# Moving the act, att, u and squares tiles by 32 and 160 bytes in SBUF, in a two-block transformer kernel

## What is computed

```python
x = first_block(x, ...)
for l in range(2):
    shift1, scale1, gate1, shift2, scale2, gate2 = split(silu(c) @ ada_w[l] + ada_b[l])
    z = (rms_norm(x) * (1 + scale1) + shift1) @ w_in[l]
    mixed = (g_attn * y_attn + g_conv * y_conv) @ w_out[l]
    x = x + (1 + gate1) * mixed
    f_gate, f_up = split((rms_norm(x) * (1 + scale2) + shift2) @ w_ffn_in[l])
    x = x + (1 + gate2) * ((silu(f_gate) * f_up) @ w_ffn_out[l])
```

## Time and profile before

| what | value |
|---|---|
| median of 3 runs | 1083.2 us |
| the three runs | 1083.2, 1084.77, 1076.28 us |
| the profiled execution | 1082.7 us |
| its span, first to last instruction | 1080.7 us |
| mean granted TensorE clock | 0.997 of full speed |

### The profile page before, as it was taken

One profiled execution on the slowest core, in us unless ns is written; L12 is line 12 of the kernel. 1 busy time (PEld: TensorE's weight loads), 2 busy tenths in 40 slices (PEclk: granted clock), 3 DMA queues, 4 the chain that ended last, 5 costly groups with the idle time before them and its releaser, 6 DMA issues.

```text
span 1080.7 us, 19232 instructions
## 1 busy us (share of the span) xinstructions
PE 1058.1 (98%) x8174; PEld 1008.1 (93%) x8174; DVE 833.2 (77%) x1117; ACT 525.7 (49%) x625; POOL 29.8 (3%) x54
## 2 busy tenths in 40 slices
PE   7999999999999999999999999999999999999998
PEld 6778899999998989989999999999898899999998
DVE  6878599988875899877888886879998676554552
ACT  6554665553434435546544343364365464444341
POOL 5000000000000010000000000000000000000000
PEclk9999999999999999999999999999999999999998
DMA  8567249789892554338599998845441556665451
GB/s 288 159 238 243 81 179 338 264 292 317 292 351 78 196 166 156 117 141 303 186 365 314 327 334 282 282 159 198 161 153 43 205 185 197 193 190 185 158 171 39
DMA packets 137473, 230.37 MB, mean 213 GB/s; under 512 B 7107, under 2 KB 60715, under 8 KB 137389
## 3 DMA queue, kind: packets, MB, share of 16 engines
q1 hardware_dynamic: 135060, 227.05, 61.8%
q0 software_dynamic: 1408, 0.79, 0.4%
q10 hardware_dynamic: 921, 1.32, 0.4%
HBM read 227.29 MB, written 1.06 MB: 211 GB/s over the span
## 4 chain that ended last, share of the span: by engine, by line
PE 72%; DVE 18%; ACT 7%; DMA 2%; issue 1%; SPq 0%; ACTq 0%; DVEq 0%
PE mm L437 67%; DVE lo L1298 7%; DVE cacc L1388 5%; ACT hi L842 3%; PE mm L480 1%; ACT pB L921 1%; DMA raw<-in_w_out_dram 1%; DVE sB L1396 1%; DVE qk L1415 1%; DVE hf L1413 1%; DMA swap<-qk 1%; DVE qk L1414 1%; PE pv L578 1%; DMA raw<-in_w_in_dram 1%; PE pa L544 0%
## 5 line engine op out<-in xcount | busy, mean ns | idle before, releaser
L437 PE MATMUL mm<-act_hi,hi 128*128 128x256 f32 x1760 | 489.8, 282 | 5.0 <-ACT act_hi L910 2.3
L437 PE MATMUL mm<-act_hi,lo 128*128 128x256 f32 x1760 | 484.4, 279 | 0.0
L437 PE MATMUL mm<-act_lo,hi 128*128 128x256 f32 x1760 | 467.6, 279 | 0.0
L1298 DVE TENSOR_TENSOR lo<-raw,hi 128x2048 fp32r<-128x2048 f32 (+1 forms) x159 | 359.6, 2265 | 131.6 <-ACT hi L842 128.8
L842 ACT ACTIVATE hi<-raw 128x2048 fp32r<-128x2048 f32 (+1 forms) x159 | 300.2, 1891 | 245.6 <-PE mm L437 205.0
L437 PEld LDWEIGHTS mm<-act_hi,hi 128*128 128x128 f32 x1760 | 330.2, 188 | 10.0 <-issue 6.4
L437 PEld LDWEIGHTS mm<-act_hi,lo 128*128 128x128 f32 x1760 | 329.9, 187 | 0.3
L437 PEld LDWEIGHTS mm<-act_lo,hi 128*128 128x128 f32 x1760 | 320.3, 188 | 0.0
L437 PE MATMUL mm<-u_hi,hi 128*128 128x256 f32 x608 | 170.5, 280 | 0.0
L437 PE MATMUL mm<-u_lo,hi 128*128 128x256 f32 x608 | 169.9, 279 | 0.0
L437 PE MATMUL mm<-u_hi,lo 128*128 128x256 f32 x608 | 169.7, 279 | 0.0
(11 more groups left out here) (280 smaller groups left out, 907.9 us busy)
## 6 DMA issues: line engine op xcount, KB each, us to landing
ada_raw<-in_ada_w_dram SPq DMA_DIRECT2D x128, 384.0 KB, 5.1
raw<-in_w_ffn_in_dram SPq DMA_DIRECT2D x88, 512.0 KB, 5.3
raw<-in_w_in_dram SPq DMA_DIRECT2D x39, 1024.0 KB, 5.1
raw<-in_w_ffn_out_dram SPq DMA_DIRECT2D x20, 1024.0 KB, 6.3
raw<-in_w_up_dram SPq DMA_DIRECT2D x16, 1024.0 KB, 5.8
raw<-in_w_down_dram SPq DMA_DIRECT2D x16, 1024.0 KB, 7.6
raw<-in_w_out_dram SPq DMA_DIRECT2D x12, 1024.0 KB, 6.8
raw<-in_w_in_dram SPq DMA_DIRECT2D x16, 512.0 KB, 6.0
```

The lines of the kernel that those rows point to most:

```text
L437: ins = pe.matmul(o, w[:, kk, fs], a[:, k, :], start=(k == 0 and i == 0 and f % 2 == 0), stop=(ends and i == len(pairs) - 1), skip_group_c ...
L1298: v(dve.tensor_tensor(lo[:, c % RING, 0:nk, :], raw[:, c % RING, 0:nk, :], hi[:, c % RING, 0:nk, :].bitcast(F32), ALU.subtract), "lo_done")
```

## The change

One padding tile grows from 16 to 24 float32 numbers (64 to 96 bytes), and a new one of 28 numbers (112 bytes, which the rounding to 32 bytes makes 128) stands ahead of the region that `qk1`, the `mixA` and `mixB` tiles, `u_hi` and `u_lo` share:

```diff
         x = sb("x", [P, KD, S])
-        sb("act_pad", [P, 16])
+        sb("act_pad", [P, 24])
         act_hi = sb("act_hi", [P, KD, S], F32R)
         act_lo = sb("act_lo", [P, KD, S], F32R)
...
         tabs = sb("tabs", [P, 2, 2 * S])
 
 
+        sb("mix_pad", [P, 28])
         mixA = ExitStack()
         qk1 = sb("qk1", [P, KD, S], on=mixA)
```

## The result

| what | before | after |
|---|---|---|
| median | 1080.85 us (4 runs, 1076.28 to 1084.77) | 1094.76 us (4 runs, 1094.3 to 1096.2) |
| profiled execution, its span | 1082.7, 1080.7 us | 1094.55, 1092.4 us |

The ratio after to before is 1.0132, with a 95% interval of 1.0086 to 1.0179: the changed kernel is slower, by 1.3%. It lies inside the stated range, but not where the forecast was, which was no change. One more thing stands in the table: the kernel before scatters over 8.5 us, the changed one over 1.9 us.

The account below looks back on a forecast made before the run. The prediction took TensorE's issue pace at L437 to bound the kernel. Every moved tile was costed at 0, so 1082.7 + 0 = 1082.7 us for the profiled execution; it named 1082, range 1050 to 1104.

Parts of the forecast that it names:

- What bounds the kernel: TensorE's issue pace at line L437, about 117.8 ns between starts, 67% of the chain, 724 us; other engines' traffic changes nothing.
- I take 0 ns per matmul for all of them: Matmuls on the moved act, u and att tiles: the new starts add 0 ns each, bounded by 10 less or 7 more.
- The row of `on` at 544: Float32 product at L437, tile at 544 mod 1024: 216 ns beside 215.6 for constants, taken as sign that such starts cost nothing.
- The two paces at one address: L437's stretches: 117.8 or 113.4 ns with one layout, each stretch keeping the pace it begins with; a step of 4.4 ns.
- The slower rival: L437's float32r streams: a start not a multiple of 64 costs 4.4 ns each, 27 us, giving 1109 us; chance 0.23.
- The faster rival: L437: the new offset makes 113.4 ns the common pace, saving 25.7 us, giving 1057 us; chance 0.31 including act alone.
- That only the act tiles profit: L437: act matmuls gain, u and att nothing; 17 us saved, 1066 us; part of the faster case's 0.31.
- The inference from a rule of the Trainium skill: TensorE's two independent SBUF read ports: by that rule no layout changes the pace, and the sum is 0.
- its likeliest part, 1074 to 1088: Whole kernel: the time range for the case of no layout effect alone; chance 0.46.

Follow-up runs that it names:

- e1: Kernel before with only act and squares tiles moved, to 96 bytes past a multiple of 1024, u and att kept at 64; 1094.92 us.
- e2: Kernel before with only the shared region (u, att and the rest) moved, to 224 past a multiple of 1024, act at 64; 1087.07 us.
- e4: Kernel before with act at 0, u and att at 32 past a multiple of 1024, weights at 0; 1092.71 us.
- e6: Kernel before with act at 32, u and att at 128 past a multiple of 1024; 1083.51 us.
- b1: Separate kernel, TensorE alone: bursts of 48 float32r products with the streamed tiles at starts from 0 to 992; 119.8 to 120.0 ns a product at 96.
- e8: Kernel before with act at 256, u and att at 480 past a multiple of 1024; 1095.01 us.
- e3: Kernel before with weights, ada, x, act and u all moved by 32 bytes, so their distance stays 64; 1078.18 us.
- e5: Kernel before with act at 224, u and att at 96: the changed kernel's two starts swapped; 1091.78 us.
- b2: Separate kernel of bursts as in b1, with the starts of a_hi, a_lo and lo varied independently; 113.5 to 122.1 ns a product over 256 bursts.
- b3: Separate kernel of bursts as in b1, at start 64 or 192, each begun in ten ways; at 192, 113.3 or 113.4 ns, or 117.8 ns.
- c1: Kernel before with act, squares, u, att and all the shared region at 192, weights at 0; 1072.78 us, ratio 0.9872 to the kernel before.
- c2: The same kernel as c1 measured once more, 12 runs; 1071.98 us, ratio 0.9921 to the kernel before.

## Why the prediction was wrong

**What bounds the kernel: right.** L437's pace was the one number that mattered, and no other engine's work changed.

**The step that failed** is "I take 0 ns per matmul for all of them". The act tiles cost 120.0 - 117.8 = 2.2 ns (e1), the u and att tiles 0.55 ns (e2). Over all products that is 5280 x 2.2 = 11.7 us and 1920 x 0.55 = 1.1 us. On top, the stretch that had gone at 113.3 ns, about 520 distances in the before's profile, no longer does: 520 x 4.4 = 2.3 us. Together 15.1 us, of which the span shows 11.7 and the medians 13.9. PE's busy time grew by 14.8 us; that the rest of it fell where TensorE wasn't on the chain fits the chain (72% before, 89% after), and was not followed product by product.

**Why I took 0.** The row of `on` at 544, a float32 product, was weighed as evidence about alignment. The prediction itself said that it could not exclude an effect where stream and load are equally long; that is just the case in question, and the row should have carried no weight. Besides, 544 is 32 modulo 256, a distance at which float32r is no slower than at 64 either (e4, e6). The other argument, that all k-tiles and ring slots run at one pace, was no argument either: they are 1024 and 8192 bytes apart, multiples of the 256 bytes that count (b1, e8), so they all had the same distance.

**The two paces at one address** were read rightly as something that a stretch keeps, and the scatter of the before with them: the second long piece went at 117.8 in its profile and at 113.3 in e3's at an equal distance. What the step missed is that the set of paces, not only the choice, belongs to the distance. At 96 only 120.0 was seen (119.8 to 120.0 in b1), at 224 only 118.3 (118.2 to 118.4); the changed kernel's small scatter, 1.9 us over four runs, fits that.

**The slower rival** had the place and the sign right and the cause wrong. It priced one step at 4.4 ns, 1109 us; measured is half of that for act and an eighth for u, and 335 records in a window where it wanted 330. A start that is no multiple of 64 is not what costs (e3, e4). **The faster rival's** notion, that a larger distance avoids a collision, holds for 192 and fails for 96, 128 and 224: it is not a matter of larger. **That only the act tiles profit** asked whether 96 and 224 are alike. They are not (e5), but the act tiles lose the more, and the modulus is 256.

**The inference from a rule of the Trainium skill** failed with it. The Trainium skill, "TensorE: Matmul & The Clock Gate", section "Step-by-step: what each phase is for", says that a weight load takes no read bandwidth from the running matmul. The prediction concluded from it that no layout changes the pace. For float32r streams with a new load for each product that does not hold here: with everything else idle, b1's bursts differ by 6.6 ns a product with the distance between the two operands, and in b2 moving `lo`, which only the weight load reads, from 0 to 64 changes the pace from 119.8 to 117.8 ns (both act tiles at 0). The measurement decides; whether it is bandwidth that the load takes, no run shows.

The range held the time; its likeliest part, 1074 to 1088, did not.

## What to carry to other kernels

Where TensorE loads new weights for every product of 256 float32r columns, the distance of the streamed tile from the stationary tile, modulo 256 bytes, can be worth 1 to 2%: here the same kernel took 1072 us with act and u at 192 and 1097.55 us with both at 96. Measure it in a kernel of bursts first, and pad for it. With one distance for all streamed tiles 192 was best and 0 and 96 worst; 112, with 114.1 to 114.5 ns in b1, was not tried in the full kernel. Before a row is used as evidence that a layout doesn't matter, ask whether the positions that it compares differ modulo the period at all, and read the distance between starts, not the duration of a record: PE was 98% busy at every one of these paces.

## What was not expected of the hardware

- The pace of such a stream is one of a few fixed values for its distance (113.3, 117.8, 118.3 and 120.0 ns are the most frequent), and it holds for 1500 products in a row (e3). At several distances, 32, 64, 160 and 192 among them, two were seen, and for 32, 64 and 192 what ran ahead selects one (b1, b3). It accounts for the 8.2 us between the profiles of c1 and c2, one program; what selects it in the full kernel was not tried. That it is also behind the before's whole spread of 17 us is likely, but only one of those runs has a profile.
- The token-major form (512 columns streamed, act stationary) depends on the start too: 233.3 ns in the mean at 64, 234.0 at 96, 229.6 at 192, 227.5 at 0 and 256, where the other form is at its worst.
- That the two reads collide in SBUF is argued, not shown: no run looked inside, and none streamed float32r without new weights or loaded weights without a stream. What is shown is that the distance of the two operands counts while moving both by 32 bytes changes nothing (e3, the only common shift tried), that the paces repeat every 256 bytes (b1, e8), and that it takes TensorE alone (b1).
